# Triangular inversion of an RWKV-7 scan: the lower levels moved from 64x64 to 32x32 array tiles

## The reference, cut to what matters

```
def step(s, inp):
    r_t, w_t, k_t, v_t, kk_t, b_t = inp
    sa = einsum('bhvk,bhk->bhv', s, kk_t)
    s = s * w_t - sa[..., None] * b_t + v_t[..., None] * k_t
    y = einsum('bhvk,bhk->bhv', s, r_t)
    return s, y
s_f, y_f = wkv_scan(..., reverse=False)
s_b, y_b = wkv_scan(..., reverse=True)
```

## Time and profile before

| what | value |
|---|---|
| median of 3 runs | 3016.3 us (3009.99 to 3019.97) |
| profiled execution, its own time | 3018.82 us |
| its span in the trace | 3016.4 us |
| scan's pairs, first inversion matmul to last `fin` (trace, 457 to 1137 us) | 680.0 us |
| PE busy in these 680 us | 572.39 us |
| granted clock there | 0.96 |

### The profile page before, as it was taken

One profiled execution on the slowest core, in us unless ns is written; L12 is line 12 of the kernel. 1 busy time (PEld: TensorE's weight loads), 2 busy tenths in 40 slices (PEclk: granted clock), 3 DMA queues, 4 the chain that ended last, 5 costly groups with the idle time before them and its releaser, 6 DMA issues. The chain is left out here.

```text
span 3016.4 us, 75964 instructions
## 1 busy us (share of the span) xinstructions
PE 2721.9 (90%) x33244; PEld 2404.6 (80%) x33244; DVE 1158.6 (38%) x3005; ACT 577.9 (19%) x1471; POOL 564.9 (19%) x571
## 2 busy tenths in 40 slices
PE   7999958887878897967999999999999999999991
PEld 2555527787877883437999999999999999999991
DVE  1388565555564443334213321232223221332125
ACT  4010153343442332320000100011000100010002
POOL 0683024434445331000000000000000000000002
PEclk9999978898999999978999999999999999999996
DMA  5522210000001004017687777777687768777753
GB/s 206 166 98 84 84 40 7 3 4 7 4 6 38 6 5 179 28 50 294 258 315 266 266 265 275 280 282 271 242 317 281 269 243 316 266 266 264 276 210 133
DMA packets 235260, 517.97 MB, mean 172 GB/s; under 512 B 9854, under 2 KB 42878, under 8 KB 234939
## 3 DMA queue, kind: packets, MB, share of 16 engines
q1 hardware_dynamic: 224410, 483.14, 43.8%
q0 software_dynamic: 8176, 21.83, 3.0%
q10 hardware_dynamic: 2480, 10.06, 0.8%
HBM read 488.68 MB, written 26.33 MB: 171 GB/s over the span
## 5 line engine op out<-in xcount | busy, mean ns | idle before, releaser
L2313 PE MATMUL ps_h<-xT,w1c 128*128 128x144 f32 x4096 | 547.3, 287 | 1.3 <-ACT xT L2119 1.3
L2313 PE MATMUL ps_h<-xT,w3c 128*128 128x144 f32 x4096 | 544.4, 287 | 0.0
L2313 PEld LDWEIGHTS ps_h<-xT,w1c 128*128 128x128 f32 x4096 | 520.5, 191 | 1.7 <-ACT xT L2119 1.7
L2313 PEld LDWEIGHTS ps_h<-xT,w3c 128*128 128x128 f32 x4096 | 519.9, 191 | 0.0
L2323 PE MATMUL ps_ye<-he,w2c 128*128 128x144 f32 x4096 | 512.3, 286 | 0.0
L2323 PEld LDWEIGHTS ps_ye<-he,w2c 128*128 128x128 f32 x4096 | 505.9, 191 | 0.0
L2268 DVE TENSOR_TENSOR u<-ps_h,sig 128x144 f32<-128x144 f32 x256 | 78.7, 307 | 888.7 <-ACT sig L2150 888.7
L563 PE MATMUL front_bank<-wide,win 128*128 128x384 f32 x912 | 298.1, 489 | 2.0 <-DVE wide L447 2.0
L2150 ACT ACTIVATE sig<-ps_h 128x144 f32<-128x144 f32 x256 | 74.3, 290 | 1065.9 <-PE ps_h L2313 1065.9
L563 PEld LDWEIGHTS front_bank<-wide,win 128*128 128x128 f32 x912 | 173.8, 191 | 127.3 <-issue 9.2
L2181 POOL DMA_INDIRECT acc<-ys,idx_s x16 | 25.8, 1615 | 1002.8 <-ACT ye_p L2139 872.0
(11 more groups left out here) (284 smaller groups left out, 3146.1 us busy)
## 6 DMA issues: line engine op xcount, KB each, us to landing
w1c<-in_w SPq DMA_DIRECT2D x64, 2048.0 KB, 8.0
w3c<-in_w SPq DMA_DIRECT2D x64, 2048.0 KB, 13.0
w2c<-in_w SPq DMA_DIRECT2D x64, 2048.0 KB, 13.2
ada<-in_ada_w SPq DMA_DIRECT2D x24, 1024.0 KB, 6.1
prow<-probsT ACTq DMA_DIRECT2D x17, 576.0 KB, 7.1
win<-in_w_in SPq DMA_DIRECT2D x19, 512.0 KB, 3.9
z<-in_x_all SPq DMA_DIRECT2D x3, 1536.0 KB, 13.9
acc<-zero SPq DMA_DIRECT2D x9, 512.0 KB, 7.0
```

Source lines behind the costliest of these rows:

```text
L2313: ins = eng.matmul(ps_h[g % 2][:, off:off + SLOTS], w[:, b, k, f * P:(f + 1) * P], xT[:, k], start=(k == 0), stop=(k == KT - 1))
```

## The change

The lower levels (0 to 4) work on the four 32x32 diagonal quarters of a chunk pair, `Q[c][i]`, in place of the two 64x64 halves `H[c]`: below level 5 T, TT and X are block-diagonal with blocks of 32, so the zeros between them are left out. `tw` and `xw` hold the compact blocks only (32 columns in place of 64), and the PSUM bank holds T, TT (256 columns) and X (128 columns) side by side. Level 0 makes both T and TT on TensorE, by a matmul with the identity each, so that ACT copies both in one instruction and POOL's wait for that copy goes. At the last level X has one 32x32 block per matrix; a new step, `inv_own`, puts the two diagonal blocks of TT and a zero block into PSUM by matmuls with the identity, `inv_t` adds the off-diagonal block, and DVE copies the whole TT to a new tile `tf`, from which `wu` reads.

The diff, without the sizes of `Q` and the last lines on `tf`:

```diff
-    tw = sb("tw", [P, 2, 4, 2, CH])
-    xw = sb("xw", [P, 2, 4, CH])
+    tw = sb("tw", [P, 2, 4, 2, QS])
+    xw = sb("xw", [P, 2, 4, QS])
+    tf = sb("tf", [P, 2, 4, CH])
...
-            eng.activation(tw[:, b, :, 0], INV[b][:, 0:4 * CH].rearrange("p (u c) -> p u c", u=4), ACT.Copy).then_inc(t0_s[b], 1)
-
-        def begin_tt(n):
-            b = n % 2
-            eng.wait_ge(lm_p[b], levels_done(n, 0))
-            eng.activation(tw[:, b, :, 1], lm[:, b, 0], ACT.Copy).then_inc(t0_s[b], 1)
+            eng.activation(tw[:, b].rearrange("p u k c -> p (u k c)"), INV[b][:, 0:4 * CH], ACT.Copy).then_inc(t0_s[b], 1)
...
-            eng.activation(xw[:, n % 2].rearrange("p u c -> p (u c)"), INV[n % 2][:, 0:4 * CH], ACT.Copy).then_inc(x_s[n % 2], 1)
+            eng.activation(xw[:, n % 2].rearrange("p u c -> p (u c)"), INV[n % 2][:, 4 * CH:6 * CH], ACT.Copy).then_inc(x_s[n % 2], 1)
...
-                ins = eng.tensor_tensor(flat, INV[b][:], flat, ALU.add)
+                ins = eng.tensor_tensor(flat, INV[b][:, 0:4 * CH], flat, ALU.add)
             else:
-                eng.wait_ge(t_pe[b], (n // 2) * LAST + lv)
-                ins = eng.tensor_tensor(tw[:, s, :, 1], INV[b][:].rearrange("p (u k c) -> p u k c", u=4, k=2)[:, :, 1],
-                                        tw[:, s, :, 1], ALU.add)
+                if n >= 2:
+                    eng.wait_ge(wu_pe, n - 1)
+                ins = eng.tensor_copy(tf[:, s].rearrange("p u c -> p (u c)"), INV[b][:, 0:4 * CH])
...
         def inv_x(n, lv):
...
+            if lv == 0:
+                for u in range(4):
+                    for k in range(2):
+                        for c in range(2):
+                            for i in range(2):
+                                own, e = lm[Q[c][i], b, 0, u, HALF[i]], eye[Q[c][i], HALF[i]]
+                                ins = mm(tt[Q[c][i], u, k], *((own, e) if k == 0 else (e, own)))
+            elif lv < LAST:
+                for u in range(4):
+                    for c in range(2):
+                        for i in range(2):
+                            ins = mm(x[Q[c][i], u], lm[Q[c][i], b, lv % 2, u, HALF[i]], tw[Q[c][i], s, u, 0])
+            else:
+                for u in range(4):
+                    j = u // 2
+                    i = 1 - j
+                    for c in range(2):
+                        ins = mm(x[Q[c][i], u], lm[Q[c][j], b, lv % 2, u, HALF[i]], tw[Q[c][j], s, u, 0])
+            ins.then_inc(x_pe[b], 1)
+
+        def inv_own(n):
+            b = s = n % 2
+            whole = INV[b][:, 0:4 * CH].rearrange("p (u c) -> p u c", u=4)
+            eng.wait_ge(x_s[b], (n // 2) * LAST + LAST)
             for u in range(4):
+                j = u // 2
                 for c in range(2):
-                    ins = mm(INV[b][H[c], u * CH:(u + 1) * CH], lm[H[c], b, lv % 2, u],
-                             tw[H[c], s, u, 0] if lv else eye[H[c]])
-            ins.then_inc(x_pe[b], 1)
+                    for i in range(2):
+                        ins = mm(whole[Q[c][i], u, HALF[i]], eye[Q[c][i], HALF[i]], tw[Q[c][i], s, u, 1])
+                    i = 1 - j
+                    ins = mm(whole[Q[c][i], u, HALF[j]], eye[Q[c][i], HALF[i]], eye[Q[c][i], HALF[j]])
+            ins.then_inc(t_pe[b], 1)
...
         def inv_t(n, lv):
...
-            for u in range(4):
-                if lv < LAST:
+            if lv < LAST:
+                tt = INV[b][:, 0:4 * CH].rearrange("p (u k c) -> p u k c", u=4, k=2)
+                for u in range(4):
+                    for k in range(2):
+                        for c in range(2):
+                            for i in range(2):
+                                q = Q[c][i]
+                                ins = mm(tt[q, u, k], *((tw[q, s, u, 1], xw[q, b, u]) if k == 0 else (xw[q, b, u], tw[q, s, u, 1])))
+            else:
+                whole = INV[b][:, 0:4 * CH].rearrange("p (u c) -> p u c", u=4)
+                for u in range(4):
+                    j = u // 2
+                    i = 1 - j
                     for c in range(2):
-                        mm(INV[b][H[c], 2 * u * CH:(2 * u + 1) * CH], tw[H[c], s, u, 1], xw[H[c], b, u])
-                for c in range(2):
-                    ins = mm(INV[b][H[c], (2 * u + 1) * CH:(2 * u + 2) * CH], xw[H[c], b, u], tw[H[c], s, u, 1])
+                        ins = mm(whole[Q[c][j], u, HALF[i]], xw[Q[c][i], b, u], tw[Q[c][i], s, u, 1])
             ins.then_inc(t_pe[b], 1)
...
                     spot(p, 2)
+                    inv_own(a)
+                    inv_own(b)
                 inv_t(a, lv)
                 inv_t(b, lv)
```

More of the change, by code:

```diff
@@ L601, in scan_phase @@
     NB = NTOK // P
+    QS = CH // 2
     def const(name):
@@ L686, in scan_phase @@
     H = (slice(0, HS), slice(HS, P))
+    Q = [[slice(c * CH + i * QS, c * CH + (i + 1) * QS) for i in range(2)] for c in range(2)]
+    HALF = (slice(0, QS), slice(QS, CH))
     NCELL = CT * NB
@@ L889, in level @@
             b, k = n % 2, n // 2
-            if lv == 2:
-                eng.wait_ge(t0_s[b], 2 * k + 2)
             if lv >= 2:
@@ L1051, in begin_t @@
             b = n % 2
-            if n >= 2:
-                eng.wait_ge(wu_pe, n - 1)
             eng.wait_ge(x_pe[b], (n // 2) * LEVELS + 1)
-            eng.activation(tw[:, b, :, 0], INV[b][:, 0:4 * CH].rearrange("p (u c) -> p u c", u=4), ACT.Copy).then_inc(t0_s[b], 1)
-        def begin_tt(n):
-            b = n % 2
-            eng.wait_ge(lm_p[b], levels_done(n, 0))
-            eng.activation(tw[:, b, :, 1], lm[:, b, 0], ACT.Copy).then_inc(t0_s[b], 1)
+            eng.activation(tw[:, b].rearrange("p u k c -> p (u k c)"), INV[b][:, 0:4 * CH], ACT.Copy).then_inc(t0_s[b], 1)
         def take_x(n, lv):
             eng.wait_ge(x_pe[n % 2], (n // 2) * LEVELS + lv + 1)
-            eng.activation(xw[:, n % 2].rearrange("p u c -> p (u c)"), INV[n % 2][:, 0:4 * CH], ACT.Copy).then_inc(x_s[n % 2], 1)
+            eng.activation(xw[:, n % 2].rearrange("p u c -> p (u c)"), INV[n % 2][:, 4 * CH:6 * CH], ACT.Copy).then_inc(x_s[n % 2], 1)
         def take_n(n):
@@ L1141, in _ @@
             begin_t(a + 1)
-            begin_tt(a)
             if old:
                 take_wu(old[1])
-            begin_tt(a + 1)
             for lv in range(1, LEVELS):
@@ L1274, in take_t @@
             b = s = n % 2
+            eng.wait_ge(t_pe[b], (n // 2) * LEVELS + (lv if lv < LAST else LEVELS))
             if lv < LAST:
                 if lv == 1:
-                    eng.wait_ge(t0_s[b], 2 * (n // 2) + 2)
-                eng.wait_ge(t_pe[b], (n // 2) * LAST + lv)
+                    eng.wait_ge(t0_s[b], n // 2 + 1)
                 flat = tw[:, s].rearrange("p u k c -> p (u k c)")
-                ins = eng.tensor_tensor(flat, INV[b][:], flat, ALU.add)
+                ins = eng.tensor_tensor(flat, INV[b][:, 0:4 * CH], flat, ALU.add)
             else:
-                eng.wait_ge(t_pe[b], (n // 2) * LAST + lv)
-                ins = eng.tensor_tensor(tw[:, s, :, 1], INV[b][:].rearrange("p (u k c) -> p u k c", u=4, k=2)[:, :, 1],
-                                        tw[:, s, :, 1], ALU.add)
+                if n >= 2:
+                    eng.wait_ge(wu_pe, n - 1)
+                ins = eng.tensor_copy(tf[:, s].rearrange("p u c -> p (u c)"), INV[b][:, 0:4 * CH])
             ins.then_inc(t_v[b], 1)
@@ L1485, in inv_x @@
             b = s = n % 2
+            tt = INV[b][:, 0:4 * CH].rearrange("p (u k c) -> p u k c", u=4, k=2)
+            x = INV[b][:, 4 * CH:6 * CH].rearrange("p (u c) -> p u c", u=4)
             eng.wait_ge(lm_p[b], levels_done(n, lv))
@@ L1490, in inv_x @@
             elif lv == 1:
-                eng.wait_ge(t0_s[b], 2 * (n // 2) + 1)
+                eng.wait_ge(t0_s[b], n // 2 + 1)
             else:
                 eng.wait_ge(t_v[b], (n // 2) * LAST + lv - 1)
+            if lv == 0:
[16 more added lines that the diff above has]
+                        ins = mm(x[Q[c][i], u], lm[Q[c][j], b, lv % 2, u, HALF[i]], tw[Q[c][j], s, u, 0])
@@ L1500, in inv_t @@
         def inv_t(n, lv):
             b = s = n % 2
-            eng.wait_ge(x_s[b], (n // 2) * LAST + lv)
-            if lv == 1:
-                eng.wait_ge(t0_s[b], 2 * (n // 2) + 2)
-            for u in range(4):
-                if lv < LAST:
+            if lv < LAST:
+                eng.wait_ge(x_s[b], (n // 2) * LAST + lv)
+            else:
+                eng.wait_ge(t_pe[b], (n // 2) * LEVELS + LAST)
+            if lv < LAST:
+                tt = INV[b][:, 0:4 * CH].rearrange("p (u k c) -> p u k c", u=4, k=2)
+                for u in range(4):
[4 more added lines that the diff above has]
+                                ins = mm(tt[q, u, k], *((tw[q, s, u, 1], xw[q, b, u]) if k == 0 else (xw[q, b, u], tw[q, s, u, 1])))
+            else:
+                whole = INV[b][:, 0:4 * CH].rearrange("p (u c) -> p u c", u=4)
+                for u in range(4):
+                    j = u // 2
```

(3 more changed lines are left out.)

## The result

The change makes the kernel slower: 3231.9 us (median of 4 runs, 3226.33 to 3235.35) against 3013.14 us for the kernel before in the same session (4 runs, 3009.57 to 3019.97), a ratio of 1.0718 with a 95% interval of 1.0703 to 1.0733. The profiled execution took 3230.93 us, 212 more than the profiled one before.

A forecast was written before the change was run, and what follows sets the result against it. TensorE was taken as held about equally by its work and by its instruction packets; 869 us of packets + 15 clock and unevenness + 25 waits = 909 us stage, 229 more than 680, so 3248 us, range 3145 to 3350 (chance 0.80).

The forecast's parts named there:

- The bound: Scan stage: PE held about equally by its work and by instruction packets, with a stop every 255 instructions.
- The price of a packet: PE's instruction supply in the stage: 3.82 us for a packet, from eight timed packets (30.53 / 8).
- the 869 us of the term: PE's instructions in the stage: 227.4 packets in place of 146, at 3.82 us each.
- the rest: Stage time beside the packets: 15 us for clock and unevenness, 25 us for waits on other engines.
- closer than 3 would have been a sign of being wrong: Stage's instruction packets: spacing under 3 us would show the prediction wrong.
- This term does not enter the sum: Inversion matmuls: a packet's 127 take 1.0 to 3.7 us, under 3.82, so PE's work there adds nothing.
- The clock: Stage's other matmuls: a lower granted clock could make them dearer; 15 us with unevenness, between 0 and 75.
- slower by more: Rival, stage: packets at 4.15 us and clock low for a third or longer; 3399 us, 3350 and up; chance 0.08.
- Waits: PE's waits for other engines in the stage: 25 us taken, bounds 0 and the 41.2 us of before.
- DVE's shorter adds: DVE's 144 adds: 425 ns in place of 691, 38 us less work, costed at nothing, hidden by PE's stream.
- A sign that missed: Sign of being right: PE's busy share in the stage under 0.7, with "issue" its largest wait by far.
- The page: Skill page on instruction fetch: boundary cost mostly hidden, so 81 packets would cost nothing; the prediction held the trace disagrees.

The follow-up runs named there:

- the loop: Kernel before plus series behind the scan's last matmul, each a hardware loop of 80 rounds: 5120 recorded 32x32 matmuls take 78.7 us; whole kernel 4398.95 us.
- bare series: Kernel before plus 2560 program matmuls on 32x32 tiles, written out behind the scan's last matmul: 142.5 us for 39 packets; whole kernel 4423.1 us.
- the written-out 64x64 series: Kernel before plus 2560 program matmuls on 64x64 tiles, written out behind the scan's last matmul: 153.4 us for 40 packets; whole kernel 4423.1 us.
- filler kernel: Kernel before plus 144 unread 32x32 matmuls per cell, as many added instructions as the change, without its new dependencies: 3239.41 us, ratio 1.0746.

## Why the prediction was right

**The bound.** That PE's stops are those of its instructions, a packet apart, held: the stops go up with the packets, and the loop, which needs none, takes 78.7 us for what takes 142.5 written out.

**The count.** 227.4 packets were predicted and 227 came.

**The price of a packet.** The prediction took 3.82 us from eight windows of before. The bare series has 3.65 us on the mean, and by that the 869 us of the term were 227 x 3.65 = 829, 40 too many, and the rest, predicted at 15 + 25 = 40 us, is 892 - 829 = 63. The stage itself gives another price: the windows above range from 3.64 to 4.01, 19.48 / 5 = 3.90 on the mean, and in the trace's own records of the queue the 227 packets start 3.79 us apart at the median, never less than 3.29 (closer than 3 would have been a sign of being wrong). At 3.79 the term is 860 and the rest 32. By the bare series two errors nearly cancel in the 909 us predicted for the 892 measured, by the stage's own price both terms are 8 or 9 too large; which of the two holds is not shown, and so it stays open how much of the closeness is luck. Two of the windows in the earlier trace rows may also have held PE by its work for a part, as the written-out 64x64 series, which does not stop, takes 3.84 us for a packet.

**Work.** "This term does not enter the sum" held: the filler kernel has 108 us more work on PE and the same length. The 32x32 matmuls are 8.9 ns apart in the loop, inside the 7.8 to 15.7 taken for four tiles, and the run of 64 in the changed kernel's own timeline gives the same at full clock: (0.76 - 0.19) / 63 = 9.0 ns.

**The clock.** The condition of the rival "slower by more" came true, its price did not. The mean of 0.78 means (1 - 0.78) / 0.5 = 44% of the stage at the lower level, where the rival asked for a third and put 75 us on it. The filler kernel at 0.97 is no quicker: a stage that waits for its packets has the time for slower matmuls.

**Waits.** Those for other engines are 17 us where 25 were taken. The reading under that term was short: the prediction called them a small part of before, 41.2 us in three rows, but all rows add up to 53, half of PE's 108 idle us. DVE's shorter adds take 425 ns as forecast and bought little here, if anything: the filler kernel has the long ones, and its stage is 6 us longer.

**A sign that missed.** PE's busy share was to fall under 0.7, and is 0.74. The slower matmuls at the lower clock count as busy and cover a part of each stop (in the bare series the same 128 are busy for 1.28 us early on and for 1.93 at 0.50); "issue" is therefore not the whole price of the supply either, as the filler kernel shows (109 us, same length).

**The page.** The Trainium skill, "Runtime: NRT & Kernel Launch", section "Instruction fetch mechanics", calls the cost of a block's boundary mostly hidden. In the bare series 1.81 of 3.74 us is PE standing still at the boundary, and 81 blocks made 212 us here; on 64x64 tiles, where a block's work takes 3.84 us, it is hidden as the page says.

What sets 3.65 us for a packet was not tried and stays open.

## What to carry to other kernels

Count the instructions of written-out TensorE code beside its busy time: where 256 of them (in float32 64 program matmuls) do less than some 3.7 us of work, the packets set the pace, and smaller tiles in more instructions make it slower, as here. The price of a packet more rises in the table from 1.3 us (130 to 146 packets) to about 3 (from 167 up); fewer and larger instructions for the same result (a 128x128 transposition for four matmuls with the identity) bring that back, and a loop escaped it in the bare series. A saving on one engine that is paid with many small instructions on the next is to be priced there too.

## What the runs showed that was not expected

An instruction that holds nothing but two waits on a semaphore that is already met costs TensorE's queue 98 to 112 ns, as much as eleven matmuls on 32x32 tiles. And the granted clock fell where PE stood still for much of the time: the 32x32 series, written out, began at 1.00 and ran at 0.50 from its second stop on, and in the loop, with gaps of 0.24 us, it stayed at 1.00. Stops alone do not bring the clock down, as the filler kernel has 152 waits without a name and 0.97; what does was not tried.
